# The row of 1/rms at both feed-forward norms, and six unread matmuls before the second up products

## What is computed

```python
# first block, D_MODEL = 2048, FFN_HIDDEN = 5632, SEQ = 256
h = rmsnorm(x, g_pre_ffn) * (1.0 + scale2) + shift2
gu = h @ w_ffn_in                       # 2048 x 11264
g_ffn, u_ffn = split(gu, 2)
y = (silu(g_ffn) * u_ffn) @ w_ffn_out
x = x + gate2 * rmsnorm(y, g_post_ffn)
...
# second block
h = rms_norm(x, norm_ffn_w)
u = causal_depthwise_conv(h @ w_ffn_up, w_ffn_conv, b_ffn_conv)
u_gate, u_val = split(u, 2)
x = x + (gelu(u_gate) * u_val) @ w_ffn_down

def rms_norm(x, w):                     # the mean is over the 2048 features of a token
    return x * rsqrt(mean(x * x, axis=-1) + EPS) * w
```

## Time and profile before

| what | before |
|---|---|
| median of 3 runs | 2794.21 us |
| the profiled execution, its device time | 2796.14 us |
| the profiled execution, its span | 2794.4 us |
| TensorE busy | 2725.7 us (98%) |
| VectorE busy | 1820.3 us (65%) |
| ScalarE busy | 1290.2 us (46%) |
| share of the chain that ended last: PE | 89% |
| share of DVE in that chain | 7% |
| mean granted TensorE clock | 0.991 |

### The profile page before, as it was taken

The page is one execution under the profiler, slowest core; times in us unless marked ns, Lnnn a source line. Parts: engine busy times, 40 slices in busy tenths (PEclk is TensorE's granted clock), DMA queues, the critical chain, the costliest instruction groups (busy, mean ns, idle before and its releaser), DMA issues.

```text
span 2794.4 us, 38988 instructions
## 1 busy us (share of the span) xinstructions
PE 2725.7 (98%) x14835; PEld 2346.2 (84%) x14835; DVE 1820.3 (65%) x2017; ACT 1290.2 (46%) x1555; POOL 290.6 (10%) x161
## 2 busy tenths in 40 slices
PE   4899999999999999999999999999999999999998
PEld 4798888788888888888888989878888888888887
DVE  7966779689955556655567544656666654666555
ACT  2256554334444444444444444535555533555454
POOL 3010122100000100000100000100113110131100
PEclk8899999999999999999999999999999999999999
DMA  9975646698935567755566654445555565555553
GB/s 373 353 258 195 224 152 215 227 326 305 340 127 193 180 203 249 254 181 188 187 222 244 216 166 151 161 145 180 182 185 190 180 201 190 192 184 194 182 199 131
DMA packets 299522, 588.70 MB, mean 211 GB/s; under 512 B 12282, under 2 KB 19438, under 8 KB 298510
## 3 DMA queue, kind: packets, MB, share of 16 engines
q1 hardware_dynamic: 292816, 577.84, 61.0%
q10 hardware_dynamic: 6590, 9.27, 1.0%
HBM read 584.98 MB, written 2.10 MB: 210 GB/s over the span
## 4 chain that ended last, share of the span: by engine, by line
PE 89%; DVE 7%; issue 2%; ACT 1%; DMA 1%; SPq 0%; POOL 0%; DVEq 0%; POOLq 0%; ACTq 0%
PE psum L781 13%; PE psum L785 13%; PE psum L783 13%; PE bank L974 12%; PE psum L974 12%; PE bank L977 6%; PE psum L977 6%; PE psum L792 2%; PE psum L796 2%; PE psum L794 2%; DVE ada_acc L865 2%; DVE mod_acc L652 2%; DVE w_lo L739 2%; PE bank L2647 1%; PE bank L947 1%
## 5 line engine op out<-in xcount | busy, mean ns | idle before, releaser
L739 DVE TENSOR_TENSOR w_lo<-raw,w_hi 128x1024 fp32r<-128x1024 f32 x912 | 1165.3, 1293 | 836.7 <-ACT w_hi L727 825.7
L727 ACT ACTIVATE w_hi<-raw 128x1024 fp32r<-128x1024 f32 x912 | 953.6, 1054 | 1269.4 <-PE psum L785 568.4
L974 PE MATMUL psum<-h_both,w_hi 128*128 128x512 f32 x1408 | 495.1, 395 | 0.8 <-DVE x L2415 0.7
L974 PE MATMUL bank<-h_both,w_hi 128*128 128x512 f32 x1408 | 493.8, 395 | 0.0
L977 PE MATMUL bank<-h_both,w_lo 128*128 128x256 f32 x1408 | 394.8, 280 | 0.0
L977 PE MATMUL psum<-h_both,w_lo 128*128 128x256 f32 x1408 | 394.8, 280 | 0.0
L781 PE MATMUL psum<-w_hi,h_both 128*128 128x512 f32 x880 | 348.6, 396 | 0.8 <-ACT tokbuf L1826 0.7
L785 PE MATMUL psum<-w_hi,h_both 128*128 128x512 f32 x880 | 343.5, 390 | 0.0
L783 PE MATMUL psum<-w_lo,h_both 128*128 128x512 f32 x880 | 343.4, 390 | 0.0
L974 PEld LDWEIGHTS psum<-h_both,w_hi 128*128 128x128 f32 x1408 | 264.0, 187 | 62.7 <-DVE x L2415 1.0
L974 PEld LDWEIGHTS bank<-h_both,w_hi 128*128 128x128 f32 x1408 | 263.9, 187 | 61.9
(11 more groups left out here) (369 smaller groups left out, 3188.5 us busy)
## 6 DMA issues: line engine op xcount, KB each, us to landing
raw<-in_w_in_dram SPq DMA_DIRECT2D x120, 1024.0 KB, 5.2
raw<-in_w_ffn_in_dram SPq DMA_DIRECT2D x88, 1024.0 KB, 5.0
raw<-in_w_ffn_up_dram SPq DMA_DIRECT2D x88, 1024.0 KB, 5.0
raw<-in_w_ada_dram SPq DMA_DIRECT2D x64, 1024.0 KB, 5.2
raw<-in_w_ffn_out_dram SPq DMA_DIRECT2D x44, 1024.0 KB, 5.2
raw<-in_w_ffn_down_dram SPq DMA_DIRECT2D x44, 1024.0 KB, 5.1
ada_raw<-in_w_ada_dram SPq DMA_DIRECT2D x64, 512.0 KB, 8.0
raw<-in_w_out_dram SPq DMA_DIRECT2D x32, 1024.0 KB, 5.3
```

Source lines behind the costliest of these rows:

```text
L727: nc.scalar.activation(w_hi[:, slot, :, 0:ncol], raw[:, rs, 2 * h:2 * h + 2, 0:ncol], ACT.Copy).then_inc(split_hi, inc)
L739: nc.vector.tensor_tensor(w_lo[:, slot, :, 0:ncol], raw[:, rs, 2 * h:2 * h + 2, 0:ncol], w_hi[:, slot, :, 0:ncol].bitcast(F32), ALU.subtra ...
L974: pe.matmul(region[:, f, :].rearrange("p (s t) -> p s t", s=2), w_hi[:, slot, kk, cols_], h_both[:, :, k, :], start=first, stop=False, ski ...
```

## The change

Four things change.

1. At norm1 and norm3 the pairs are turned by the plain transpose. Three pairs are turned early (at norm1 between two stretches of unread matmuls, 18 and 14 where 44 stood; at norm3 ahead of `proj_products`). When 1/rms is there, `r_row_pe` makes the row in bank 3 from the broadcast statistics and the identity, DVE copies it to `r_row`, and only then the fourth pair may be turned into bank 3. DVE multiplies each tile by the gain column and the row into `tmp`. At norm1 ACT adds the shift and rounds, and DVE takes the remainder with the shift; at norm3 ACT rounds a copy of `tmp` and DVE subtracts.
2. At norm1 the remainder of weight half 3 is taken behind the residual steps, where it stood ahead of them.
3. At norm2 the unread matmuls write bank 3 where they wrote bank 0, and the row is made by `r_row_pe`; nobody makes diag there.
4. Ahead of the loop of up1_1 PE waits for the same semaphore that its first products wait for and then runs six matmuls of 128 columns that nobody reads.

PE at norm1, from the last matmuls of the mixer's output on, before. Line 997 is the unread matmuls, 947 the products with diag, 974 and 977 the up products.

```diff
@@ bank_uses
-        ("norm1", (2, 2, 2, 2)), ("up1_0", (FFN_PARTS[0][1],) * 4), ("mod_down0", (0, 0, 0, 2)),
+        ("r_row1", (0, 0, 0, 1)), ("norm1", (2, 2, 2, 2)), ("up1_0", (FFN_PARTS[0][1],) * 4), ("mod_down0", (0, 0, 0, 2)),
...
-        ("norm3", (2, 2, 2, 2)), ("up2_0", (FFN_PARTS[0][1],) * 4),
+        ("r_row3", (0, 0, 0, 1)), ("norm3", (2, 2, 2, 2)), ("up2_0", (FFN_PARTS[0][1],) * 4),
@@ helpers of PE
+        def r_row_pe(pe, stage, b, r):
+
+            pe.wait_ge(sem("rms"), r + 1)
+            pe.wait_ge(bank_free[b], fill(stage, b))
+            for t in range(TT):
+                mm = pe.matmul(bank[:, b, t * P:(t + 1) * P], stats[:, r, 2 + t:3 + t].to_broadcast([P, P]),
+                               ident[:], start=t == 0, stop=t == TT - 1, skip_group_check=True)
+            mm.then_inc(bank_full[b], 1)
...
-        def keep_busy(pe, stage, n):
+        def keep_busy(pe, ready, n):
 
-            pe.wait_ge(bank_free[0], fill(stage, 0))
+            pe.wait_ge(*ready)
             for k in range(n):
-                pe.matmul(bank[:, 0, :].rearrange("p (s t) -> p s t", s=2), h_hi[:, k % KD, 0:P],
+                pe.matmul(bank[:, 3, :].rearrange("p (s t) -> p s t", s=2), h_hi[:, k % KD, 0:P],
                           h_both[:, :, k % KD, :], start=True, stop=True, skip_group_check=True)
@@ split_dve (norm3 now calls it with row=r_row)
-            if shift is not None:
+            if shift is not None or row is not None:
...
+                        if row is None:
+                            ins = nc.vector.tensor_scalar(tmp[:, b % 2, k, :], tile_, gain[:, f:f + 1],
+                                                          shift[:, f:f + 1], ALU.mult, ALU.add)
+                        else:
+                            ins = nc.vector.scalar_tensor_tensor(tmp[:, b % 2, k, :], tile_, gain[:, f:f + 1],
+                                                                 row[:], ALU.mult, ALU.mult)
@@ ACT at norm1
-            split_act(act, "norm1", h_hi, KD, a_cols[:, 1, :], mod_cols[:, 3 * KD:4 * KD], between=plan.up1[0])
+            for b in range(KD // 2):
+                if b > 4:
+                    split_w_hi(act, plan.up1[0], 0, b - 1, b)
+                act.wait_ge(sem("norm1_scaled"), b + 1)
+                for k in range(2):
+                    f = 2 * b + k
+                    nc.scalar.activation(h_hi[:, f, :], tmp[:, b % 2, k, :], ACT.Identity,
+                                         bias=mod_cols[:, 3 * KD + f:3 * KD + f + 1]).then_inc(sem("norm1_hi"), 1)
+            split_w_hi(act, plan.up1[0], 0, 7, 8)
@@ ACT at norm3
-            split_act(act, "norm3", h_hi, KD, gain_of("norm_ffn_w_2"), between=plan.up2[0], ahead=2)
+            split_act(act, "norm3", h_hi, KD, gain_of("norm_ffn_w_2"), shift=r_row, between=plan.up2[0], ahead=2)
@@ DVE at norm1
-            split_w_lo(dve, plan.up1[0], 0, 3, 4)
             dve.wait_ge(sem("x_again"), 16)
             residual_dve(dve, chain, 1)
-            normed_dve(dve, 2)
-            split_dve(dve, "norm1", h_hi, h_lo, KD, a_cols[:, 1, :], mod_cols[:, 3 * KD:4 * KD], between=plan.up1[0])
+            split_w_lo(dve, plan.up1[0], 0, 3, 4)
+            dve.wait_ge(bank_full[3], filled("r_row1", 3))
+            nc.vector.tensor_copy(r_row[:], bank[:, 3, 0:TOK]).then_inc(bank_free[3], 1)
+            dve.wait_ge(bank_free[3], emptied("r_row1", 3))
+
+            def lower1(b):
+                dve.wait_ge(sem("norm1_hi"), 2 * b + 2)
+                for k in range(2):
+                    f = 2 * b + k
+                    ins = nc.vector.scalar_tensor_tensor(
+                        h_lo[:, f, :], tmp[:, b % 2, k, :], mod_cols[:, 3 * KD + f:3 * KD + f + 1],
+                        h_hi[:, f, :].bitcast(F32), ALU.add, ALU.subtract)
+                ins.then_inc(bank_free[b % 4], 1)
+
+            for b in range(KD // 2):
+                dve.wait_ge(bank_full[b % 4], filled("norm1", b % 4, b // 4))
...
+                for k in range(2):
+                    f = 2 * b + k
+                    ins = nc.vector.scalar_tensor_tensor(
+                        tmp[:, b % 2, k, :], bank[:, b % 4, k * TOK:(k + 1) * TOK], a_cols[:, 1, f:f + 1], r_row[:],
+                        ALU.mult, ALU.mult)
+                ins.then_inc(sem("norm1_scaled"), 1)
+                if b:
+                    lower1(b - 1)
+                if b > 4:
+                    split_w_lo(dve, plan.up1[0], 0, b - 1, b)
+            lower1(KD // 2 - 1)
+            split_w_lo(dve, plan.up1[0], 0, 7, 8)
@@ DVE in the second layer's first group
-                        split_w_lo(dve, ph, 0, *span(ph, 0, part=(4, 6)))
-                        normed_dve(dve, 4)
-                        split_w_lo(dve, ph, 0, *span(ph, 0, part=(6, 8)))
+                        split_w_lo(dve, ph, 0, *span(ph, 0, part=(4, 8)))
@@ DVE at norm3
-            normed_dve(dve, 5)
             split_w_lo(dve, plan.up2[0], 0, 0, 2)
-            split_dve(dve, "norm3", h_hi, h_lo, KD, gain_of("norm_ffn_w_2"), between=plan.up2[0], ahead=2)
+            dve.wait_ge(bank_full[3], filled("r_row3", 3))
+            nc.vector.tensor_copy(r_row[:], bank[:, 3, 0:TOK]).then_inc(bank_free[3], 1)
+            dve.wait_ge(bank_free[3], emptied("r_row3", 3))
+            split_dve(dve, "norm3", h_hi, h_lo, KD, gain_of("norm_ffn_w_2"), row=r_row, between=plan.up2[0], ahead=2)
@@ PE at norm1
-            keep_busy(pe, "norm1", 44)
-            pe.wait_ge(sem("normed"), 4)
-            normed_products(pe, plan.up1[0], "norm1", 2, up="up1_0")
+            keep_busy(pe, (bank_free[3], fill("r_row1", 3)), 18)
+            for b in range(3):
+                pe.wait_ge(sem("x_ready"), 2 * (b // 2 + 1))
+                transpose_pair_pe(pe, "norm1", x, b)
+            keep_busy(pe, (bank_free[3], fill("r_row1", 3)), 14)
+            r_row_pe(pe, "r_row1", 3, 2)
+            transpose_pair_pe(pe, "norm1", x, 3)
+            for h in range(KD // 2):
+                up_products(pe, plan.up1[0], 0, 0, "up1_0", ready="norm1", part=(h, h + 1))
+                if h < 4:
+                    transpose_pair_pe(pe, "norm1", x, 4 + h)
             for part, (g0, n) in enumerate(FFN_PARTS):
                 ph = plan.up1[part]
                 if part == 0:
                     up_products(pe, ph, 0, 1, "up1_0")
+                else:
+                    pe.wait_ge(psum_free[0], ph.free(0, 0))
+                    for k in range(6):
+                        pe.matmul(psum[0][:, 0, 0:P], h_hi[:, k, 0:P], h_hi[:, k, 0:P], start=True, stop=True,
+                                  skip_group_check=True)
@@ PE at norm2
-            keep_busy(pe, "norm2", 20)
+            keep_busy(pe, (bank_free[3], fill("norm2", 3)), 20)
...
-            pe.wait_ge(sem("normed"), 6)
-            pe.wait_ge(bank_free[0], fill("r_row", 0))
-            for t in range(TT):
-                mm = pe.matmul(bank[:, 0, t * P:(t + 1) * P], ones[:], diag[:, t, :], start=t == 0,
-                               stop=t == TT - 1, skip_group_check=True)
-            mm.then_inc(bank_full[0], 1)
+            r_row_pe(pe, "r_row", 0, 4)
@@ PE at norm3
+            for b in range(3):
+                pe.wait_ge(psum_free[ph.pair[b // 2]], ph.freed(0, b // 2))
+                transpose_pair_pe(pe, "norm3", x, b)
             tile_ready(pe, "ple", 0)
             proj_products(pe, 0)
-            pe.wait_ge(sem("normed"), 8)
-            normed_products(pe, plan.up2[0], "norm3", 5, up="up2_0")
+            r_row_pe(pe, "r_row3", 3, 5)
+            transpose_pair_pe(pe, "norm3", x, 3)
+            for h in range(KD // 2):
+                up_products(pe, plan.up2[0], 0, 0, "up2_0", ready="norm3", part=(h, h + 1))
+                if h < 4:
+                    transpose_pair_pe(pe, "norm3", x, 4 + h)
```

More of the change, by code:

```diff
@@ L949, in transpose_pair_pe @@
             mm.then_inc(bank_full[b % 4], 1)
+        def r_row_pe(pe, stage, b, r):
[7 more added lines that the diff above has]
+            pe.wait_ge(*ready)
+            for k in range(n):
+                pe.matmul(bank[:, 3, :].rearrange("p (s t) -> p s t", s=2), h_hi[:, k % KD, 0:P],
+                          h_both[:, :, k % KD, :], start=True, stop=True, skip_group_check=True)
         def up_products(pe, ph, i, g, stage, ready=None, part=(0, 8)):
@@ L991, in up_products @@
                 half(idx, range(4))
-        def keep_busy(pe, stage, n):
-            pe.wait_ge(bank_free[0], fill(stage, 0))
-            for k in range(n):
-                pe.matmul(bank[:, 0, :].rearrange("p (s t) -> p s t", s=2), h_hi[:, k % KD, 0:P],
-                          h_both[:, :, k % KD, :], start=True, stop=True, skip_group_check=True)
         def normed_products(pe, ph, stage, r, transposed=False, up=None):
@@ L1052, in gained_pair_dve, with split_dve @@
             ins.then_inc(bank_free[b % 4], 1)
-        def split_dve(dve, stage, hi, lo, tiles, gain=None, shift=None, between=None, ahead=4):
```

(9 more changed lines are left out.)

2 lines of the change are left out of this document (added).

## The result

| what | before | after |
|---|---|---|
| median of 11 runs each, side by side | 2792.83 us | 2800.61 us |
| lowest and highest | 2787.49, 2800.78 | 2793.32, 2805.41 |
| ratio after/before, 95% interval | | 1.0022 [1.0012, 1.0031] |
| the profiled execution | 2796.14 us | 2805.15 us |
| its span | 2794.4 us | 2803.4 us |

The forecast was 2786.0 us with a range up to 2795.5; 2800.6 lies outside of it. It still lies inside the bounds of "same", 2785.8 and 2802.6, which the prediction gave 0.59; that the change costs time at all rests on the interval. The nearest case was the fourth rival, 2800.1, and that it came so near is partly luck: it is a sum of +4.0 on the profiled execution's 2796.1, where the profiled executions differ by +9.0.

What follows compares the result with a forecast made beforehand. PE, busy 98% of the span, was taken as the bound. From the profiled 2796.1 us, norm1 -2.6, norm3 +1.0, six matmuls +0.7, paces -4.3 and -4.9 made -10.1: 2786.0 us, range 2781.5 to 2795.5.

Steps and rivals of the forecast that it cites:

- the bounds of "same": Whole kernel: about 0.3%, 8.4 us, either side of the median can't be told from no change; chance 0.59.
- the fourth rival: Up products: up1_0 and up1_1 stay slow, up2_0 turns slow behind four transposes; +4.0, 2800.1 us; chance 0.05.
- The pace of up1_1: Start of up1_1: six unread matmuls make a different start that leads to the fast pace; -4.3 us, otherwise 0.
- The pace of up1_0, up2_0 and up2_1: Changed starts behind the norms: up1_0 turns fast, -4.9 us; up2_0 stays fast, 0; up2_1 has no term.
- behind a wait one out of one: Argument for the fast pace: the one part starting behind a 0.7 us wait was fast.
- norm1: forecast -2.6: norm1: first product -2.4, four pairs turned between halves -1.8, spell at 1.2 GHz +1.6.
- norm3: forecast +1.0: norm3: first product +1.65, four pairs between halves -1.8, slower clock in a new PE gap +1.2.
- the third rival: Clock at both norms: the low spell lasts twice as long, +1.6 us each, 2789.2 us; chance 0.07.
- norm2: forecast 0: norm2: dropping diag frees only idle DVE time, row costs PE the same, bank 3 wait 0 to 0.1 us.
- The cover that held: norm1, behind the first half: DVE's lead of some 3 us hides its extra work; 0, or 1.2 us if gone.
- second rival: Up products: paces stay as they are, 2795.2 us, or two starts slow in another pair, at most 2795.8; chance 0.13.

Runs made afterwards that it cites:

- after_four: The changed kernel with four unread matmuls instead of six ahead of up1_1; 2795.38 us, ratio to before 1.0001.
- norm3_only: The kernel before with the change at norm3 alone, without the six matmuls; 2795.31 us, ratio 1.0008.
- before_two: The kernel before with two unread matmuls of 128 columns ahead of up1_1; 2789.56 us, ratio 0.9991.
- two_nowait: The kernel before with two unread matmuls ahead of up1_1 and up2_1, and PSUM columns reordered so PE's wait at up2_1 is gone; 2784.96 us, ratio 0.9970.
- shake: The kernel before with 1, 2, 3, 4 unread matmuls ahead of groups of up1_0, up1_1, up2_0, up2_1 (except each layer's first); 2806.97 us, ratio 1.0045.
- group_before: The kernel before with up products grouped by shape, four 512-column matmuls and then four of 256, instead of alternating; 2795.15 us, ratio 1.0012.
- norm1_w_late: The kernel before with the change at norm1 and norm2 alone, weight remainder moved behind the third pair's scalings; 2797.26 us, ratio 1.0006.
- norm1_two: The kernel before with changed norm1 and norm2, weight remainder behind the third pair's scalings, and two unread matmuls at up1_1; 2788.28 us, ratio 0.9983.
- after_no_six: The changed kernel without the six unread matmuls ahead of up1_1; 2795.51 us, ratio to before 1.0018.
- group_after: The changed kernel with up products grouped by shape instead of alternating; 2795.90 us, ratio to before 1.0015.

## Why the prediction was wrong, point by point

**The pace of up1_1: the step that failed first.** "I take -4.3" for the six matmuls. The mechanism was right: unread matmuls in front of this start can turn it fast, and two or four do. But a different start was taken for another pace, and six leads back to the slow one. The term is 0, and the six cost 0.62 us (forecast 0.7). My two values, gained or nothing, were the right ends; the value between them was chosen for no row.

**The pace of up1_0, up2_0 and up2_1: the larger failure.** "... fast is likelier than slow for both: I take -4.9 and 0." The profiled run of after gave 0 and +4.9, and up2_1, which my sum did not hold at all, gave +4.2, behind the same wait of 0.7 us as before. The argument "behind a wait one out of one" rested on one execution, though the spread of 10 us between three runs was named in the text; and it read the row as a start behind a wait, where eight slow pairs stand ahead of the wait. Over the traces with alternating pairs that have no added matmuls at the start in question, up1_0 was slow in 2 of 5 with the old norm1 and 3 of 6 with the new; up2_0 in 0 of 7 with the old norm3 and 2 of 4 with the new; up2_1 in 7 of 10, and fast in the one with two unread matmuls in place of its wait. So the start at norm3 was the sure one before, and the change made a throw of it. That fits the fourth rival in part: up2_0 went slow, but after_four and norm3_only show it fast behind the same four transposes, so these don't lead to it alone. How often the unprofiled runs take which pace is not seen; that the median of after holds one or two slow parts more than that of before is worked out from 7.8 us by the medians and 5.7 by the means, and not shown.

**norm1: forecast -2.6, came -1.0.** From the stage's start to the second group it took 802.8 - 759.54 = 43.2 us where it took 804.6 - 760.36 = 44.2, both with the slow pace. In parts: the first product -1.5 (forecast -2.4; 0.9 lost to POOL beside the weight remainder), the four pairs -1.8 as forecast, and the clock +2.3 where +1.6 was taken: its 6.8 us covered eight pairs at 0.64. But the gain itself was partly one execution's: 18.12 us to the first product is what before takes with a spell of 1.2 GHz on its diag products. In before_two, two_nowait, shake, group_before and norm3_only, with the same old stage and no such spell, it is 16.65, the same as after's 16.66. Against those (42.6 to 42.7 to the second group) the new norm1 of after is 0.5 us slower. With the remainder moved away from POOL it took 42.6 in norm1_w_late (a spell of 6.8 us) and 41.5 in norm1_two (3.4 us). The prediction's own bounds for norm1 add up to -4.6 and -0.5, not -0.3; nothing hangs on it.

**norm3: forecast +1.0, came +2.3 without the pace.** The first product comes 10.69 us after the first of the stage's matmuls instead of 9.24: +1.45 (forecast 1.65). The four pairs give -1.8 back, and the clock takes 2.7, where 1.2 was taken; this is the third rival, and with norm1's 0.7 it is worth 2.2 here. It is no fixed cost: the same stage had 6.8 us at 1.2 GHz in after, 3.4 in after_no_six, norm3_only and group_after and none in after_four, whose first group takes 24.16 us against 27.16 (0.4 of the difference is the pace).

**norm2: forecast 0, came about -1.4,** since its spell of 1.2 GHz was absent in after. It is absent in most traces of either kind, so this too belongs to the one execution.

**The cover that held:** PE waits for no tile behind the first half of either norm; DVE's lead was there.

**The sum, with what came in:** -0.8 from ahead of norm1, -1.0, +2.3, +0.6, -1.4 and +9.1 for the pace make +8.8 of +9.0, all between the two profiled executions. With the pace taken out it is near zero, which fits the +0.8 of the two grouped kernels.

The rule that could have warned me of the 0.9 us is in the Trainium skill, SBUF — State Buffer, section SBUF: two separate sides: an operation of DVE with two inputs in SBUF and one of GpSimd that reads SBUF take turns at a shared pair of ports, whole instruction by whole instruction. By that rule moving the remainder behind the squares puts POOL behind it. The traces agree: 1.09 us beside it, 0.19 without.

The back-to-back rule of the Trainium skill that I set against my large terms (second rival) knows one pace. Its section gives the formula for an isolated matmul and says that in a real stream the weight loads count too, which I left out. These traces have two paces for the same pairs at the same clock, so it lost as a rule; as a forecast, paces unmoved and 2795.2, it was nearer than mine.

## What to carry to other kernels

Where a long stream of alternating matmul shapes has no gap, measure its time per pair in every part and in several executions before pricing anything smaller: here 1.9% of the pair's time hangs on the last thing that interrupted the stream, and two short unread matmuls behind gap-free work made it fast each time (four did in the one kernel tried), where six did nothing. An order without alternation gives a single pace in between and a kernel whose small changes can be measured. A small instruction on POOL must not fall beside a large two-input instruction of DVE, if anyone waits for it.

## What the runs showed of the hardware

- The starts of alternating matmuls of 512 and 256 columns settle into one of three patterns: one that repeats after each pair and one that repeats after two, both 0.3467 us a pair, and one that repeats after three, 0.3533. The 512-column records last 391 ns in the first, 392 and 395 by turns in the second, and 395, 403 and 398 in the third; their medians, 391, 394 and 398, mark the three. Grouped by shape the same matmuls take 0.350. Why there are three, and what a gap does to the choice, stays open: behind a gap of PE the same instructions led to either pace in different executions (up1_0, up2_0 with the new norm3, up2_1).
- A spell at 1.2 GHz came in lengths of 3.4, 6.8 and 10.2 us at these stages. At norm1 the old stage had 0 or 3.4 in seven traces, the new one 3.4 to 10.2 in seven; at norm3 the old stage none in nine, the new one 0 to 6.8 in five. The new stages, with more short gaps of PE and little to fill them, had more of it; which gap does it was not isolated. Whether it matters that the filling is transposes was not tried.
- POOL's first small instruction (TENSOR_SCALAR on 128 x 2 elements) takes 0.19 us alone and 1.09 to 1.10 beside DVE's 128 x 1024 remainder, and ends with it.
